# Order of VectorE and ScalarE work at five stops of a two-block transformer kernel

## Reference, cut to what matters

```python
FF = 2816
def gla(q, k, v, g_f, g_b, s_f, s_b): ...   # q·decay·k within 512 tokens, both directions, plus carried states
def diff_attend(q, k, v, lam):              # per head
    s = einsum("qcd,kcd->cqk", rope(rmsnorm(q)), cat(k_ctx, rope(rmsnorm(k)))) * 64 ** -0.5
    p = softmax(s)
    return (p[0] - lam * p[1]) @ v
def conv_ffn(h, w_up, conv_w, conv_b, w_down):      # second block
    z = h @ w_up
    zc = conv_w[2] * z + conv_w[1] * shift(z, 1) + conv_w[0] * shift(z, 2) + conv_b
    g, u = zc[..., :FF], zc[..., FF:]
    return (gelu(g) * u) @ w_down
```

## Time and profile before

| what | us |
| --- | --- |
| median of three runs | 1679.67 |
| profiled execution, whole | 1679.19 |
| its span, first to last instruction | 1677.6 |
| PE busy | 1586.2 |
| DVE busy | 933.8 |
| ACT busy | 731.2 |
| POOL busy | 124.7 |

### The profile page before, as it was taken

One profiled execution on the slowest core, in us unless ns is written; L12 is line 12 of the kernel. 1 busy time (PEld: TensorE's weight loads), 2 busy tenths in 40 slices (PEclk: granted clock), 3 DMA queues, 4 the chain that ended last, 5 costly groups with the idle time before them and its releaser, 6 DMA issues.

```text
span 1677.6 us, 19157 instructions
## 1 busy us (share of the span) xinstructions
PE 1586.2 (95%) x7606; PEld 1248.9 (74%) x7606; DVE 933.8 (56%) x1441; ACT 731.2 (44%) x1132; POOL 124.7 (7%) x89
## 2 busy tenths in 40 slices
PE   8998989798899999999999899999987899999999
PEld 2776867587688888888878677788675688888885
DVE  3665776785744433334555555366656676257743
ACT  4453435576332222223343767455455444234432
POOL 0100122531000000000010011130010000000000
PEclk9999999789999999999999999999988899999999
DMA  9441111200624233222232222143212132333231
GB/s 372 156 166 44 51 38 53 73 1 6 229 105 139 76 100 118 95 85 87 94 105 73 63 71 73 51 138 101 75 36 90 51 99 71 118 103 92 81 99 55
DMA packets 47950, 156.60 MB, mean 93 GB/s; under 512 B 5587, under 2 KB 10323, under 8 KB 47350
## 3 DMA queue, kind: packets, MB, share of 16 engines
q1 hardware_dynamic: 47280, 152.00, 27.3%
q10 hardware_dynamic: 582, 3.38, 0.6%
HBM read 153.26 MB, written 2.10 MB: 93 GB/s over the span
## 4 chain that ended last, share of the span: by engine, by line
PE 77%; DVE 13%; ACT 6%; issue 3%; POOL 0%; DMA 0%; ACTq 0%; DVEq 0%
PE pall L2076 18%; PE pall L2078 18%; PE pall L2077 18%; PE pall L2112 2%; PE pall L2113 2%; PE pall L2114 2%; PE pall L2559 1%; PE pall L2094 1%; PE pall L2095 1%; PE pall L2096 1%; PE pall L2561 1%; PE pall L2560 1%; DVE wlo L1228 1%; DVE statd L1560 1%; PE pall L2154 1%
## 5 line engine op out<-in xcount | busy, mean ns | idle before, releaser
L1228 DVE TENSOR_TENSOR wlo<-raw,whi 128x1024 fp32r<-128x1024 f32 (+2 forms) x261 | 290.3, 1114 | 314.6 <-ACT whi L559 314.6
L559 ACT ACTIVATE whi<-raw 128x1024 fp32r<-128x1024 f32 (+2 forms) x263 | 246.5, 939 | 148.5 <-PE pall L2078 113.1
L2076 PE MATMUL pall<-h5h,whi 128*128 128x512 f32 x320 | 126.2, 394 | 7.9 <-DVE wlo L1228 7.9
L2078 PE MATMUL pall<-h5h,wlo 128*128 128x512 f32 x320 | 125.7, 393 | 0.0
L2077 PE MATMUL pall<-h5l,whi 128*128 128x512 f32 x320 | 125.6, 393 | 0.0
L2078 PE MATMUL pall<-h2h,wlo 128*128 128x512 f32 x320 | 124.7, 390 | 0.0
L2076 PE MATMUL pall<-h2h,whi 128*128 128x512 f32 x320 | 124.6, 390 | 0.0
L2077 PE MATMUL pall<-h2l,whi 128*128 128x512 f32 x320 | 124.6, 389 | 0.0
L2076 PEld LDWEIGHTS pall<-h5h,whi 128*128 128x128 f32 x320 | 60.8, 190 | 21.1 <-issue 8.6
L1175 ACT ACTIVATE tmp<-pall,vec 128x512 f32<-128x512 f32 x44 | 34.1, 780 | 93.6 <-DVE pall L1881 93.6
L2077 PEld LDWEIGHTS pall<-h5l,whi 128*128 128x128 f32 x320 | 60.7, 190 | 13.0 <-issue 0.2
(11 more groups left out here) (460 smaller groups left out, 3640.1 us busy)
## 6 DMA issues: line engine op xcount, KB each, us to landing
raw<-in_weights SPq DMA_DIRECT2D x204, 512.0 KB, 3.5
mraw<-in_wmod SPq DMA_DIRECT2D x32, 512.0 KB, 5.0
mod<-in_weights SPq DMA_DIRECT2D x16, 512.0 KB, 12.0
raw<-in_weights SPq DMA_DIRECT2D x25, 256.0 KB, 2.6
raw<-in_weights SPq DMA_DIRECT2D x32, 192.0 KB, 2.3
xT<-in_x SPq DMA_DIRECT2D x1, 2048.0 KB, 16.7
xT<-in_x ACTq DMA_DIRECT2D x1, 2048.0 KB, 8.1
out_y<-xT SPq DMA_DIRECT2D x8, 256.0 KB, 2.1
```

The costliest lines, as they stand in the source:

```text
L559: e.activation(whi[j % 3][:, 0:cols(j)], raw[j % 4][:, 0:cols(j)], ACT.Copy).then_inc(s.hi, 1)
L1228: e.tensor_tensor(wlo[j % 3][:, 0:n], raw[j % 4][:, 0:n], f(whi[j % 3][:, 0:n]), ALU.subtract).then_inc(s.lo_v, 1)
L2076: e.matmul(o_, a[:, kk, :], xh(k), start=(k == 0), stop=False)
L2078: mm = e.matmul(o_, b[:, kk, :], xh(k), start=False, stop=(k == nk - 1))
```

## The change

All five places keep the same operations; two scratch banks are renamed.

1. Second feed-forward. `hi(f+3)` and `lo(f+3)` stand behind the norm's root instead of in the loop, and f+4 ahead of jj = 1. In the loop both run three pieces ahead, each call moved: on ACT behind its `conv`, on DVE it stays between `times_root` and the end of the convolution.
2. First head of the differential attention. `key_parts(0, ...)` stand earlier; the last query norm (square, sum, root, `query_norm(3)`) moves behind the heads' norms, on DVE into the attention loop. The last query tile uses bank 7 and not 0, and the sums use banks 3 and 6.
3. `level_keys(9)` stands ahead of `key_norm(3)`.
4. `keys_decayed(0)` stands ahead of the last gate.
5. On ACT, roots of the key norms stand ahead of `decays` of levels 8 and 9.

```diff
@@ -479,6 +479,11 @@
             return hp, lev, i % 2 if i < 6 else 2 + i % 2, NI * hp + max(lev - MG, 0)
 
 
+        DQ = (0, 1, 2, 7)
+        DQS = (3, 3, 6, 6)
+        HS = (3, 3, 3, 6)
+
@@ -740,12 +745,15 @@
                 if i:
                     key_squares(i - 1)
                 hi(J[("dk", i, 0)] + 2)
+                if n == 6:
+                    decays(7)
+                if i:
+                    key_roots(i - 1)
                 for k in GAPS_AT.get(n, ()):
-                    decays(k)
+                    if k != 7:
+                        decays(k)
                 if i == 0:
                     query_start(0)
-                else:
-                    key_roots(i - 1)
 
 
             def gate_r(i):
@@ -819,16 +827,16 @@
                 if i == 3:
                     out_square(2)
                 hi(J[("dq", i, 0)] + 2)
+                if i == 3:
+                    key_parts(0, 1)
                 query_root(i - 1)
-                if i == 2:
+                if i == 1:
                     w.wait_ge(s.lsub, 14)
                     key_parts(0, 0)
+            out_square(3)
             out_root(2)
-            key_parts(0, 1)
+            out_root(3)
             query_square(3)
-            out_square(3)
-            out_root(3)
-            query_root(3)
             w.wait_ge(s.lp, 4 * NI)
             e.dma_start(xT[:, :, :], ap["x"]).then_inc(s.x, 16)
 
@@ -854,6 +862,8 @@
                         w.wait_ge(s.tp, n - 2)
                         e.activation(EB[n % 3][c][:, :], bank(b, 768), ACT.Exp, bias=sd[:, col + 1:col + 2], scale=SC,
                                      accum_out=sd[:, col + 2:col + 3]).then_inc(s.ex, 1)
+                if n == 0:
+                    query_root(3)
                 if 1 <= n <= 4:
@@ -1166,6 +1176,7 @@
                     hi(J[("f2w", 2)] + 2)
             hi(J[("f2w", 6)] + 2)
             root("ffnpre", bank(at["ffnpre"]), 512, D)
+            hi(J[("f2w", 6)] + 3)
 
 
             def conv(i, b, col):
@@ -1188,14 +1199,17 @@
                 for jj in range(11 * half, 11 * half + 11):
                     if jj == 0:
                         used(("f2w", 6))
+                    if jj == 1:
+                        hi(J[("f2w", 6)] + 4)
                     if jj >= 2:
-                        hi(J[("f2g", jj, 0)] + 2)
                         used(("f2g", jj, 0))
                     conv(2 * jj, ffn_bank("f2w", ("f2g", "f2u"), 0, jj), jj)
                     if jj >= 2:
-                        hi(J[("f2u", jj, 0)] + 2)
+                        hi(J[("f2g", jj, 0)] + 3)
                         used(("f2u", jj, 0))
                     conv(2 * jj + 1, ffn_bank("f2w", ("f2g", "f2u"), 1, jj), 22 + jj)
+                    if jj >= 2:
+                        hi(J[("f2u", jj, 0)] + 3)
                     gelu(jj)
                 if half:
                     use_exp()
...
@@ -1376,18 +1397,13 @@
                 lo(J[("gv", 2 * i)] + 2)
                 if i < 2:
                     dots2(("gv", 2 * i))
+                if i == 3:
+                    keys_decayed(0)
                 gate(i)
                 if 1 <= i < 3:
                     key_gap(i - 1)
                     level_gaps(i - 1)
 
-
...
@@ -1516,8 +1531,8 @@
                     level_gaps(k)
                 lo(J[("gr", i, 0)] + 2)
                 if i == 0:
+                    level_keys(9)
                     key_norm(3)
-                    level_keys(9)
                 else:
                     level_keys(n + 1)
                     item_scores(ITEM_AT[n])
@@ -1546,12 +1561,13 @@
                     query_gap(1)
                     out_norm(1)
                 else:
+                    if i == 3:
+                        key_parts(0, 1)
                     query_norm(i - 1)
-            key_parts(0, 0)
+                    if i == 2:
+                        key_parts(0, 0)
             out_norm(2)
-            key_parts(0, 1)
             out_norm(3)
-            query_norm(3)
 
 
             def diff_max(n, c):
@@ -1591,6 +1607,8 @@
                                            ALU.add).then_inc(s.dw, 1)
                 if n < 16:
                     diff_recip(n, 0)
+                if n == 0:
+                    query_norm(3)
                 if n % 4 == 1 and n < 12:
                     key_parts(n // 4 + 1, 0)
                 if n % 4 == 2 and n < 12:
...
@@ -1939,17 +1958,19 @@
 
             for half in range(2):
                 for jj in range(11 * half, 11 * half + 11):
+                    if jj == 1:
+                        lo(J[("f2w", 6)] + 4)
                     used(("f2g", jj, 0) if jj >= 2 else ("f2w", 6))
                     times_root("ffnpre", ffn_at(jj, 0))
                     if jj < 2:
                         times_root("ffnpre", ffn_at(jj, 1))
                     if jj >= 2:
-                        lo(J[("f2g", jj, 0)] + 2)
+                        lo(J[("f2g", jj, 0)] + 3)
                     conv(2 * jj, ffn_bank("f2w", ("f2g", "f2u"), 0, jj), jj)
                     if jj >= 2:
                         used(("f2u", jj, 0))
                         times_root("ffnpre", ffn_at(jj, 1))
-                        lo(J[("f2u", jj, 0)] + 2)
+                        lo(J[("f2u", jj, 0)] + 3)
                     conv(2 * jj + 1, ffn_bank("f2w", ("f2g", "f2u"), 1, jj), 22 + jj)
                     t = tmp[2 * jj % 4][:, :]
                     w.wait_ge(s.sil, 22 + jj + 1)
@@ -2367,24 +2388,25 @@
 
 
             def query_sums(i):
-                sums(f"dq{i}", s.hnq, 8 + i + 1, bones, tmp[0], 3)
+                sums(f"dq{i}", s.hnq, 8 + i + 1, bones, tmp[0], DQS[i])
 
             for i in range(4):
-                fill(i % 3)
+                fill(DQ[i])
                 between = {2: lambda: item_at(12 + i)}
                 if i:
                     between[5 if i == 1 else 3] = lambda: query_sums(i - 1)
                 if i == 2:
                     between[7] = lambda: heads_out(1)
                 if i == 3:
-                    between[7] = lambda: sums("h2", s.hosq, 3, ones, tmp[1], 6)
-                gemm([("dq", i, 0)], [(bank(i % 3),) + x_part], x_ready, between=between)
-                freed[i % 3] = [(s.hnt, 4 + i + 1)]
-            sums("h3", s.hosq, 4, ones, tmp[1], 7)
-            query_sums(3)
+                    between[5] = lambda: sums("h2", s.hosq, 3, ones, tmp[1], HS[2])
+                gemm([("dq", i, 0)], [(bank(DQ[i]),) + x_part], x_ready, between=between)
+                freed[DQ[i]] = [(s.hnt, 4 + i + 1)]
+            sums("h3", s.hosq, 4, ones, tmp[1], HS[3])
 
 
             for n in range(21):
+                if n == 1:
+                    query_sums(3)
                 if 0 <= n - 3 < 16:
                     i = n - 3
                     b = 2 * dpair["turn", i]
```

More of the change, by code:

```diff
@@ L764, in out_root @@
                     w.wait_ge(s.hnt, (4, 0, 6, 7)[h])
-                root(f"h{h}", bank(3 if h < 2 else 4 + h), 512, 128)
+                root(f"h{h}", bank(HS[h]), 512, 128)
             def query_square(i):
@@ L769, in query_square @@
                 w.wait_ge(s.p_sum, job[f"dq{i - 1}" if i else "dk3x"])
-                e.activation(tmp[0][:, :], bank(i % 3), ACT.Square).then_inc(s.hnq, 1)
+                e.activation(tmp[0][:, :], bank(DQ[i]), ACT.Square).then_inc(s.hnq, 1)
             def query_root(i):
@@ L776, in query_root @@
                     w.wait_ge(s.hov, (1, 2, 0, 3)[i])
-                root(f"dq{i}", bank(3), 512, 64)
+                root(f"dq{i}", bank(DQS[i]), 512, 64)
             for i in range(4):
@@ L1359, in level_gaps, with keys_decayed @@
                 e.tensor_tensor(Dk[:, :, 1, :], E_[:, :, 1, :], rb, ALU.subtract).then_inc(s.lsub, 1)
+            def keys_decayed(i):
+                hp = i % 2
+                w.wait_ge(s.kde, i + 1)
+                w.wait_ge(s.dn, 4)
+                e.tensor_tensor(ktd[:, hp, 0:512], ktd[:, hp, 0:512], qk[:, hp, 1, :], ALU.mult)
+                e.tensor_tensor(ktd[:, hp, 512:768], ktd[:, hp, 512:768], kc[:, hp, :], ALU.mult).then_inc(s.kdm, 1)
             def mod_bias(m, n):
@@ L1382, in _ @@
                     level_gaps(i - 1)
-            def keys_decayed(i):
-                hp = i % 2
-                w.wait_ge(s.kde, i + 1)
-                w.wait_ge(s.dn, 4)
-                e.tensor_tensor(ktd[:, hp, 0:512], ktd[:, hp, 0:512], qk[:, hp, 1, :], ALU.mult)
-                e.tensor_tensor(ktd[:, hp, 512:768], ktd[:, hp, 512:768], kc[:, hp, :], ALU.mult).then_inc(s.kdm, 1)
             def state(i):
@@ L1430, in item_scores @@
                     e.copy_predicated(dst, m, src).then_inc(s.lat, 1)
-            keys_decayed(0)
             keys_decayed(1)
@@ L1500, in out_norm @@
             def out_norm(h):
-                newton(f"h{h}", bank(3 if h < 2 else 4 + h), 512, 128)
+                newton(f"h{h}", bank(HS[h]), 512, 128)
                 r = inv(f"h{h}")
@@ L1506, in query_norm @@
```

(5 more changed lines are left out.)

## The result

The changed kernel takes 1706.4 us (median of 4 runs, 1703.5 to 1712.1) against 1679.2 of before (1677.2 to 1679.9): ratio 1.0168, 95% interval 1.014 to 1.0196. It is 27 us slower; 1704.5 was forecast. The profiled execution is the longest of the four (1712.11 us, span 1710.5), so its trace holds some 6 us more than the median.

A forecast was written before the change was run, and what follows sets the result against it. PE, busy 95% of the span, was taken to bound the kernel. Early edits -3.6 and -9.8, first head +2.8 and second feed-forward +35.9 sum to +25.3 on 1679.2: 1704.5 us, range 1689 to 1713.

The forecast's parts named there:

- The steady pair: Second feed-forward loop: each subtraction waits for ACT's copy, 1.98 us later, twice a pair; pair grows from 10.89 to 12.59 us.
- The halves: Second feed-forward: PE late by 13.7 us in the first half, 17.0 in the second, plus 5.2 for low clock: +35.9.
- What PE would show: PE waits 1.6 to 1.7 us in most pairs, about 8 for `cl` per half; L1590 7 to 9 us earlier.
- Decayed keys: `keys_decayed(0)` moves into DVE's wait: PE's 3.3 us go, the next turned keys' bank is late next; -3.6 us.
- Key norms and level 9: Earlier roots and `level_keys` remove PE's waits of 1.40, 1.25 and 4.2 us and a low clock: -9.6 to -9.8 us.
- First head: Differential attention: scores start earlier, but the last query norm comes 2.8 us later and delays POOL, then DVE: +2.8 us.
- The sum: Whole kernel: -3.6 - 9.8 + 2.8 + 35.9 = +25.3 us, giving 1704.5 us; chance 0.72.
- Rival 1: Subtractions in the second feed-forward are not held because ACT runs ahead: 1658 us; chance 0.04.
- rival 3: Second feed-forward is neutral, its stop merely moving by a piece; only the early stops count: 1668.6 us; chance 0.04.
- Rival 2: A reserve of three pieces absorbs lateness, used up after four pairs, some 7 us less per half: 1690.6 us; chance 0.13.
- Rival 4: PE's clock stays low in the second feed-forward's loop, costing +50 us: 1718.6 us; chance 0.04.

The follow-up runs named there:

- ffn_only: The kernel before with only the new order of the second feed-forward: 1712.54 us, ratio 1.0195.
- banks_first: `early_only` with ACT's copies of the first turned keys put ahead of `decays(2)` instead of behind it: 1668.43 us, ratio 0.9946.
- lo_old_place: The changed kernel with DVE's two subtractions inside the second feed-forward's pairs back to two pieces ahead, ACT's copies left as changed: 1670.79 us, ratio 0.9943.
- hi_ahead: The changed kernel with ACT's two copies inside a second feed-forward pair put ahead of the `conv`, DVE left as changed: 1665.25 us, ratio 0.9912.
- early_only: The changed kernel with the second feed-forward's order put back as before, the four early edits kept: 1671.78 us, ratio 0.9955.
- dk_old_place: `early_only` with `keys_decayed(0)` put back behind the gates: 1673.06 us, ratio 0.9966.

## Why the prediction was right

**The steady pair.** The step on which the forecast stands held: the subtraction starts 2.56 us behind `times_root` (said: 2.59), the second `times_root` at 5.15 (5.17), the product at 10.46 (10.52), the next pair at 12.46 (12.59). In `ffn_only` DVE's waits for `whi` are 390.1 us in all, in before 314.6: 75.5 more over 40 pieces, 1.89 each (1.98). The 2.17 us are not all of DVE's idle time in the pair, as the prediction has it: there are 0.70 ahead of `cl`. These wait for ACT's `ch` behind the product and move with it, so the sum is right without them.

**The halves.** First half: the second half's first `times_root` stands at 1482.73 in before and at 1497.88 after, 15.2 later, and the stage had begun 1.6 sooner (1276.01 against 1277.57): +16.7, clock included, against 13.7 + 2.6. Second: the other 17.8 of stretch D, against 17.0 + 2.6. Together 34.5 against 35.9; measured by itself, in `ffn_only`, 33.1. The clock's share was of the size said: 36 matmuls at the slow pace against 12 are 24 x (0.43 - 0.227) = 4.9 us (5.2), 2.8 of them in the first half and 2.0 in the second.

**What PE would show.** 1.6 to 1.7 us of waiting in most pairs was forecast; 12 of 20 pairs have one, 1.30 was listed, while a pair lengthened by 1.57. Most of the difference in length is in how a wait is counted: PE's last matmul ahead of it is drawn with 0.39 us, but in the stream one takes 0.227. From 1364.90 to 1366.59 are 1.69 us, 1.46 more than a step. The Trainium skill, Perfetto Trace Analysis, section "Tensor Engine Instruction (MATMUL, LD_WEIGHTS)", says that a matmul's end is estimated from the instruction's size and not observed; the trace agrees, as matmuls drawn with 0.39 us start every 0.227. So PE's idle times read too small here. Not as forecast was the first L1590 (L1606 now), 6.5 us sooner (316.38 against 322.88) and not 7 to 9; and the new stop of 4.18 us stands ahead of the item, none ahead of the second turn.

**Decayed keys, -3.6: wrong.** Stretch A shows nothing of it. The failing step is "what is late next is the bank that the next turned keys need": what is late next is the item ahead of them, which needs the same two banks sooner. `banks_first` shows it: with the banks cleared first, 4.9 us come.

**Key norms and level 9, -9.8: right,** -8.8 in stretch A, in which the decayed keys are worth nothing. PE's waits of 1.40, 1.25 and 4.23 us are gone, and so is the low clock behind the last of them; no run takes the two edits apart. A small wait of 0.65 us for the first scores took the place of the 4.2.

**First head, +2.8: right in sign and path, perhaps small.** 3.6 us in B, 1.2 in the gains on before. The term covers POOL's chain; the second pair's exponentials behind the same norm were left out.

**The sum.** Forecast +25.3, measured +27.2 in the medians. That it is so near is in part luck, as errors cancel. Measured by themselves, the early edits bring 7.7 us and not 10.6 (decayed keys 3.6, key norms and first head about 1 each too good), and the second feed-forward costs 33.1 and not 35.9.

**Rivals.** Rival 1 (not held) and rival 3 (neutral) fall with the 1.87 and 1.85 us. Rival 3 is what `lo_old_place` shows when the hold is taken away, 1670.8 us against the 1668.6 worked out for it. Rival 2 (a reserve of three pieces) saves nothing in the changed kernel. In the first half DVE is late before one can form. In the second half there is one, used up in the fifth pair (1552.86), much as rival 2 has it; but PE then waits 7.08 us for `cl`, as it waits 7.10 in the first half, because `cl` comes at the end of DVE's own chain, which no reserve of PE shortens. In `hi_ahead` the reserve is what takes 5.2 us off the first stop. Rival 4 (low clock in the loop) falls: 1.00 over 83 us with six waits in them.

## What to carry to other kernels

When work is asked for sooner in program order, look at what releases it on the engine that makes it, not only at whether its inputs are there: a subtraction placed ahead of `conv` on one engine and its copy behind `conv` on the other costs 1.9 us each time, against at most 0.4 when copy and `times_root` are released by the same event. If a stop is removed, ask which banks its result now fills sooner and who clears them. A stop at a loop's start is to be mended by an order that also holds in the steady pair; compute that pair first.

## What the runs showed of the hardware

Short, regular stops did not lower TensorE's clock in this loop: six of 0.86 to 1.32 us, 12.47 apart, leave it at 1.00, while stops of 4.43, 4.18 and 7.1 us are followed by matmuls at the 1.2 GHz level. It holds for this loop alone: in the attention of the same execution the granted clock was 0.50 from 404.5 to 407.5 us, and no wait of PE in the 20 us ahead was longer than 1.44. The Trainium skill, TensorE: Matmul & The Clock Gate, section "A second HAM failure mode: psum-queue depth-cycling", tells of a kernel in which frequent small idle times made the clock oscillate; in this loop the trace shows no such thing.

The order of instructions isn't all: the same order gave a stretch B between 182.4 and 184.3 us. Its mean granted clock was 0.90 in the two shortest (`early_only`, `hi_ahead`) and 0.89 in the two longest (the changed kernel, `lo_old_place`), but 0.88 in `dk_old_place` with 182.5, so the clock's mean alone does not account for the length. Nor does a stop's length settle what the clock does: the stop of 2.6 us near 940 us was followed by some 7 us at the low level in one execution of the changed kernel, and stands in all other profiled executions without that; why stays open.
